# A hybrid attention and convolution layer on one core: the two partial sums of the modulation reach TensorE unjoined

## What is computed

```python
c_act = jax.nn.silu(c)
shift, scale, gate = jnp.split(c_act @ w_ada + b_ada, 3, axis=-1)
h = rms_norm(x, norm_w) * (1.0 + scale) + shift
proj = h @ w_in                      # 1024 x 2816
# proj is split: 8 query and 2 key/value heads, a gate, a GLU pair, a gate
y_a = sliding_window_attention(q, k, v, sinks) * silu(gate_a)
y_b = causal_convolution_branch(u) * silu(gate_b)
out = x + gate * (concat(y_a, y_b) @ w_out)
```

## Time and profile before

| | us |
|---|---|
| time, median of 3 runs | 427.06 (427.05, 427.06, 427.63) |
| the profiled execution, its own time | 427.99 |
| the profiled execution, its span | 426.2 |
| TensorE matmul busy | 402.5 |
| TensorE weight loads busy | 323.7 |
| VectorE busy | 337.7 |
| ScalarE busy | 212.4 |
| GpSimd busy | 113.4 |

### The profile page before, as it was taken

The page is one execution under the profiler, slowest core; times in us unless marked ns, Lnnn a source line. Parts: engine busy times, 40 slices in busy tenths (PEclk is TensorE's granted clock), DMA queues, the critical chain, the costliest instruction groups (busy, mean ns, idle before and its releaser), DMA issues.

```text
span 426.2 us, 5891 instructions
## 1 busy us (share of the span) xinstructions
PE 402.5 (94%) x2090; PEld 323.7 (76%) x2090; DVE 337.7 (79%) x562; ACT 212.4 (50%) x488; POOL 113.4 (27%) x150
## 2 busy tenths in 40 slices
PE   0799999999999999999999999899999999999996
PEld 0477778888888887877776776678788888888886
DVE  1889769799999989999989999799987895222222
ACT  3677774023310268779788988414265883100000
POOL 1400050002502444335423609973031005100000
PEclk9999999999999999999999999999999999999999
DMA  7999641817920000022021857994646059941111
GB/s 267 358 321 344 256 146 28 279 38 168 250 45 2 6 7 8 7 77 80 0 60 40 153 87 108 153 96 84 113 89 111 2 202 273 256 107 49 51 49 49
DMA packets 54326, 51.39 MB, mean 121 GB/s; under 512 B 19271, under 2 KB 49275, under 8 KB 54298
## 3 DMA queue, kind: packets, MB, share of 16 engines
q1 hardware_dynamic: 38256, 41.50, 30.8%
q0 software_dynamic: 15904, 9.44, 16.8%
q10 hardware_dynamic: 138, 0.09, 0.1%
HBM read 46.82 MB, written 4.19 MB: 120 GB/s over the span
## 4 chain that ended last, share of the span: by engine, by line
PE 52%; DVE 23%; POOL 6%; ACT 3%; issue 3%; DMA 1%; DVEq 0%; ACTq 0%; POOLq 0%
PE pm L783 4%; PE pm L573 4%; PE pm L784 4%; PE pm L785 4%; PE pm L575 4%; PE pm L574 4%; PE pm L852 4%; PE pm L851 4%; PE pm L853 4%; DVE cacc L1333 3%; PE tr L852 3%; PE tr L851 3%; PE tr L853 3%; POOL wts L440 2%; PE ps L708 2%
## 5 line engine op out<-in xcount | busy, mean ns | idle before, releaser
L573 PE MATMUL pm<-h,wts 128*128 128x512 f32 x200 | 79.8, 399 | 0.8 <-DVE gb L1466 0.8
L575 PE MATMUL pm<-h,wts 128*128 128x512 f32 x200 | 77.9, 390 | 0.0
L574 PE MATMUL pm<-h,wts 128*128 128x512 f32 x200 | 77.9, 390 | 0.0
L927 ACT ACTIVATE wts<-raw 128x1024 fp32r<-128x1024 f32 x30 | 31.2, 1051 | 35.2 <-PE pm L575 11.0
L573 PEld LDWEIGHTS pm<-h,wts 128*128 128x128 f32 x200 | 37.5, 188 | 11.1 <-issue 2.4
L783 PE MATMUL pm<-wts,h 128*128 128x256 f32 (+1 forms) x128 | 45.1, 352 | 0.1
L575 PEld LDWEIGHTS pm<-h,wts 128*128 128x128 f32 x200 | 37.5, 188 | 8.0
L574 PEld LDWEIGHTS pm<-h,wts 128*128 128x128 f32 x200 | 37.6, 188 | 7.5 <-issue 0.2
L784 PE MATMUL pm<-wts,h 128*128 128x256 f32 (+1 forms) x128 | 43.1, 337 | 0.0
L785 PE MATMUL pm<-wts,h 128*128 128x256 f32 (+1 forms) x128 | 43.1, 337 | 0.0
L440 POOL DMA_DIRECT2D wts<-in_w_in x22 | 28.8, 2699 | 50.6 <-ACT wts L929 50.6
(11 more groups left out here) (221 smaller groups left out, 925.6 us busy)
## 6 DMA issues: line engine op xcount, KB each, us to landing
slab<-in_w_ada SPq DMA_DIRECT2D x16, 512.0 KB, 8.0
raw<-in_w_in SPq DMA_DIRECT2D x14, 512.0 KB, 5.5
xs<-in_x SPq DMA_DIRECT2D x8, 512.0 KB, 10.0
raw<-in_w_ada SPq DMA_DIRECT2D x8, 512.0 KB, 4.3
xr<-in_x SPq DMA_DIRECT2D x8, 512.0 KB, 5.2
out<-xr SPq DMA_DIRECT2D x15, 256.0 KB, 2.0
wts<-in_w_in POOLq DMA_DIRECT2D x6, 512.0 KB, 8.0
raw<-in_w_in SPq DMA_DIRECT2D x8, 256.0 KB, 7.5
```

What stands on the lines that cost most here:

```text
L573: pe.matmul(out, hi_w, hi_x, start=first, stop=False)
L574: pe.matmul(out, lo_w, hi_x, start=False, stop=False)
L575: return pe.matmul(out, hi_w, lo_x, start=False, stop=last)
L927: act.activation(whalf(i, 0), src, ACT.Copy).then_inc(a_hi, 1)
```

## The change

VectorE's join goes, with its wait for VectorE's own sixth sum. TensorE multiplies both partial sums by the ones and adds in PSUM: four matmuls a block in place of two, each part's two as one accumulation group. All counts of `d_ada` become six a block, and TensorE and SyncE wait for the sixth.

```diff
         def sums_done(k, i):
-            return 7 * k + i + 1
+            return 6 * k + i + 1
...
                 if q >= 2:
-                    sp.wait_ge(d_ada, sums_done(2 * q - 3, 6))
+                    sp.wait_ge(d_ada, sums_done(2 * q - 3, 5))
...
-                pe.wait_ge(d_ada, sums_done(k, 6))
+                pe.wait_ge(d_ada, sums_done(k, 5))
                 for part in range(2):
-                    last = pe.matmul(ada_bank(k)[:, part:part + 1], ada_acc[:, k % 2, 0, part, :], ones[:, 0:1],
-                                     start=True, stop=True)
+                    for a in range(2):
+                        last = pe.matmul(ada_bank(k)[:, part:part + 1], ada_acc[:, k % 2, a, part, :], ones[:, 0:1],
+                                         start=(a == 0), stop=(a == 1))
                 last.then_inc(p_ada, 1)
...
-                if cts[-1] == KT - 1:
-                    dve.wait_ge(d_ada, sums_done(k, 5))
-                    dve.tensor_tensor(ada_acc[:, k % 2, 0, :, :], ada_acc[:, k % 2, 0, :, :], ada_acc[:, k % 2, 1, :, :],
-                                      ALU.add).then_inc(d_ada, 1)
```

## The result

The changed kernel takes 430.64 us (median of 5 runs, 430.40 to 431.49) against 427.17 us (median of 5, 427.05 to 427.67): the ratio is 1.0078, with a 95% interval of 1.0063 to 1.0092. By the medians it is slower by 3.47 us, where +0.15 was forecast. The profiled execution took 431.09 by its own time and has a span of 429.3 us, against 427.99 and 426.2.

A forecast was written before the change was run, and what follows sets the result against it. The prediction took TensorE (matmuls busy 94% of the span) as the bound, with VectorE nearly as full in the loop. Loop 0.0 plus start 0.15 gave +0.15 us on the 427.06 median: 427.2 us, range 426.3 to 428.0.

The forecast's parts named there:

- The price of the pairs: TensorE's column groups: four extra pairs of weight load and one-column matmul cost 0.43 to 0.44 us a block.
- The weight loads' share: TensorE in a full step: loads take 3.04 of 3.60 us, by which rule the extra pairs could cost nothing.
- The loop: Early loop on TensorE: removed waits of 2.09 us against 2.64 us of added weight loads, predicted as no change.
- The prediction's steps: TensorE's loop: a step that waits for nothing takes 4.10 us, the sixth, without transposes behind it, 3.75.
- the term of 0.0: The early loop's contribution to the forecast sum: 0.0 us.
- timed the sums: VectorE's partial sums in the loop: claimed ready in time, taking 2.46 + 0.68 us a step without a join.
- The start: Blocks 0 and 1 to the first transposes: added pairs delay TensorE by 0.15 us, with the clock rising near 17.9.
- Rival 2: At the start, the clock rises late, after about 19: some 1.9 us lost, 429.1 us; chance 0.08.
- Its counter-argument: At the start: the long dummy matmuls keep their length, given as evidence against a late clock rise.
- The upper bound of 0.64: At the start: with all pairs slow and the dummies still 1.58 us, the transposes come 0.64 us late.
- What follows moves only as a whole: Everything behind the first 48 us: claimed to shift as one, with no change of its own.
- Rival 4: Behind a tied loop: drift as a transfer or GpSimd step meets its neighbour otherwise, up to 1 us either way; chance 0.10.

The follow-up runs named there:

- e15: The kernel before, unchanged, run once more with a profile: 426.92 us in one execution.
- e13: The kernel before with sixteen throw-away one-column matmuls (64 TensorE instructions) ahead of block 0's columns: 428.15 us, ratio 1.0018.
- e2: The kernel before with four matmuls a block for blocks 2 to 7 only, blocks 0 and 1 still joined: 428.63 us, ratio 1.0025.
- e5: The changed kernel, unaltered, run again: 430.53 us, ratio 1.0056.
- e6: The changed kernel with four dummy matmuls ahead of block 0's columns and four instead of one and a half behind block 1's: 428.57 us, ratio 1.0033.
- e8: The changed kernel with block 1's columns moved behind all the dummy matmuls: 428.98 us, ratio 1.0045.
- e10: The kernel before with unjoined sums for blocks 2 to 7 and the last output tile unsplit, keeping program length: 428.92 us, ratio 1.0031.
- e12: The changed kernel with block 1's columns behind all dummy matmuls and a tiny VectorE instruction where each join was: 428.70 us, ratio 1.0023.
- e16: The kernel before with four matmuls a block for blocks 2 to 7 only, repeated with a profile: 428.51 us in one execution.
- e18: The changed kernel with six dummy matmuls ahead of block 0's columns and three behind block 1's, no throw-away instructions: 428.13 us, ratio 1.0026.
- e11: The kernel before with block 1's columns moved behind all the dummy matmuls: 427.42 us, ratio 0.9996.
- e9: The kernel before with four throw-away one-column matmuls (16 TensorE instructions) at the end of TensorE's program: 427.27 us, ratio 1.0005.
- e14: The kernel before with four throw-away one-column matmuls (16 TensorE instructions) ahead of block 0's columns: 428.57 us, ratio 1.0023.
- e1: The kernel before with four matmuls a block for blocks 0 and 1 only, blocks 2 to 7 still joined: 429.77 us, ratio 1.0048.
- e7: The kernel before with four dummy matmuls ahead of block 0's columns and four instead of one and a half behind block 1's: 428.27 us, ratio 1.0017.
- e3: The changed kernel with four dummy matmuls of 512 columns ahead of block 0's columns: 428.50 us, ratio 1.0015.
- e17: The changed kernel with four dummies and 36 throw-away TensorE instructions ahead of block 0's columns, three dummies behind block 1's: 429.23 us, ratio 1.0038.
- e4: The kernel before with the joins of blocks 2 to 7 moved from VectorE to GpSimd: 429.69 us, ratio 1.0048.

## Why the prediction was wrong, point by point

**The price of the pairs: right.** Eight pairs take 0.81 to 0.89 us in the loop (32.69 to 33.50, 28.50 to 29.39), so four more cost 0.38 to 0.46, where 0.43 to 0.44 was taken. The weight loads' share, which would have had them free, misled, as the trace of before said.

**The loop: right against the execution that was read, not against the other.** Steps take 4.10 to 4.17, the first waiting 0.26, as foretold, and with the loop's pairs alone the loop is +0.06 (34.73 against 34.67). But the 34.67 holds a wait that the second trace of the kernel before (e15) has not. In the first, ScalarE's conversion waits for a weight tile, VectorE for the conversion, and the last columns for VectorE, 0.94 us. ScalarE's list before the change:

```profile
42.07 1.06 ACT L927 ACTIVATE wts<-raw 128x1024 fp32r<-128x1024 f32 x1 [0.56 <-DMA raw<-in_w_in]
```

In e15 the tile is there in time. VectorE's and TensorE's lists:

```profile
42.49 1.22 DVE L1261 TENSOR_TENSOR wts<-raw,wts 128x1024 fp32r<-128x1024 f32 x1
```

```profile
46.69 0.58 PE L567 MATMUL ps<-ones,ada_acc 128*128 128x1 f32 x4 [0.42 <-DVE ada_acc L1246]
49.03 1.30 PE L602 MATMUL pm<-h,wts 128*128 128x512 f32 x5
```

The three long waits are 1.55 us there, not 2.09, and the loop is 34.15 (e13 has the same). The prediction's steps, from e15's second one at 29.41, give 29.41 + 4 x 4.10 + 3.75 = 49.56 for step 7, 0.53 later than e15's 49.03. Measured loops with the pairs are 0.51 to 0.66 longer than 34.15 (34.66 to 34.81 in e2, e5, e6, e8, e10, e12, e16, e18). By these rows the term of 0.0 took a late transfer's wait for the kernel's own; which of the two executions is the usual one is open.

The step also timed the sums as if every slab lay there. With the joins kept, waits of 0.32, 0.43, 1.00, 1.08 and 1.37 us for the slab (e11, e9, e14, e1, e7) make loops of 34.56, 34.71, 35.24, 35.34 and 35.63, each 34.15 and the wait and about 0.1. With the pairs, waits up to 1.16 leave the loop at 34.33 to 34.81 (the eight and e3), and 1.39 and 1.49 make 35.11 and 35.18 (the changed kernel, e17). So the pairs leave VectorE about 1 us of slack, with which they hide most of a late slab, and what is over is the 0.45.

**The start: wrong, and the largest part.** The step that failed took 0.15 us between 0 and 0.64, on the sentence that the clock "rises near 17.9 again". In both profiled executions of the changed kernel it rose at 22.0 and 22.3 us, and the times of 9 of 12 executions go with that; the 0.15 measured 2.06 by the transposes of block 2. Nor was 17.9 a fixed point: with the old start it lies between 16.6 and 18.5 (before, e2, e4, e9, e10, e15, e16). Rival 2 had the mechanism and nearly the price, 1.9 us against 1.68 at the first transposes and 2.06 at block 2, but a chance of 0.08. Its counter-argument, that the long dummies keep their length, was no evidence: the dummies were broken up for 1.57 us, not for 0.71 (17.10 to 18.67; 16.93 to 17.64 in the earlier trace rows), and with the same dummies unbroken (e8) nine of ten executions were early by their times. Why executions of one program differ is open. The upper bound of 0.64 was also none, since it let the pairs be slow but kept the dummies at 1.58.

**"What follows moves only as a whole": wrong.** The stretch from 129 to 221 us grew by 0.30. The gate way grew by 0.18 (0.6 in e2), but 0.18 alone says little: with the loop's joins it lies between 21.80 and 22.48 in eight traces of nine (e13 has 22.79), with the loop's pairs between 22.11 and 23.42 in eleven. Rival 4 allowed such drift, but counted transfers and GpSimd's steps, neither the place of TensorE's instructions among the packets nor VectorE's count.

**No term for instruction packets.** The sum priced the 32 added matmuls, each with its weight load, as time on TensorE alone. Shown is that 16 throw-away instructions ahead of the loop cost 1 us in the kernel before, and 16 at its end nothing that can be told from it (e14, e9); 64 ahead cost half as much (e13). That the packet among the slabs is the link is argued from 20 traces that go together (landing 7.1 to 8.3 us without a packet among them, 8.6 to 9.8 with one) and from the miss of e13, not shown by moving a packet alone. Open: why the first packet lies at 43 us in the kernel before and near 33 in all with 16 or more added instructions ahead, and what lengthens the gate way, where the third packet at 72 to 80 us mostly goes along (22.4 to 23.4) but e9 (22.48 without one), e12 (22.11) and e18 (22.27) don't fit.

So of the 3.05 us of the two traces 2.06 are the clock's, 0.45 the loop's (the wait for the slab), 0.18 the gate way's, 0.30 VectorE's shift and 0.06 are spread. Against e15's trace the changed kernel's last output add is 4.12 us later: 2.22 at block 2, 0.96 in the loop, 0.47 in the gate way, 0.29 from 129 to 221 us and 0.18 spread. The clock is the largest part by either; the loop's part depends on the trace.

## What to carry to other kernels

Before a wait is booked as one that a change can win, look whether a second execution has it. Where TensorE works across a rise of its clock, look at the spread of the executions, and price the start at both levels all the way through, the work behind the added instructions too. Keeping the long matmuls together (e8) went with the early rise more often, not always. Before costing added instructions by engine time alone, look where the instruction packets lie in the DMA view, and whether a transfer that ends a wait shares that stretch. A tie in a loop is no gain when it is bought with instructions of the fuller engine.

## What the runs showed of the hardware

- The clock's rise isn't fixed by the program: in programs with the same TensorE work up to it, it came at 17.9 (e1), at 22.0 (e5) and at 22.3 us (after). Late groups of executions are 1.8 (e5) to 2.6 us (e1) slower. In e3 the granted clock fell to 0.50 during an idle time of 2.31 us.
- Sixteen TensorE instructions in idle time cost 1.0 us when ahead of the loop (e14, ratio 1.0023) and nothing measurable at the end (e9, 1.0005).
- Without any of the eight joins or instructions in their places, VectorE is idle for 0.26 or 0.27 us some 130 us behind them, and the stretch takes 0.3 us longer.
- GpSimd's addition of 128 by 256 float32 elements took 0.73 to 1.64 us (e4); VectorE's takes 0.42.
